# Five slots in place of eight in a ring of gathered expert rows

## The reference, cut to what matters

```python
def peer_ffn(xn, wq, keys1, keys2, u_tab, v_tab):
    q = (xn @ wq).reshape(t, PEER_HEADS, PEER_D_KEY)
    s1 = jnp.einsum('thd,hkd->thk', q[..., :half], keys1)
    s2 = jnp.einsum('thd,hkd->thk', q[..., half:], keys2)
    v1, i1 = lax.top_k(s1, PEER_TOPK)
    v2, i2 = lax.top_k(s2, PEER_TOPK)
    cand = (v1[..., :, None] + v2[..., None, :]).reshape(t, PEER_HEADS, PEER_TOPK * PEER_TOPK)
    cs, ci = lax.top_k(cand, PEER_TOPK)
    ...
    expert = e1 * PEER_N_KEYS + e2
    gate = jax.nn.softmax(cs, axis=-1)
    ...
        act = jax.nn.gelu(jnp.einsum('td,thkd->thk', xb, u_tab[eb]), approximate=False)
        return jnp.einsum('thk,thkd->td', gb * act, v_tab[eb])
```

## Time and profile before

| | |
|---|---|
| median of 3 runs | 4342.82 us (4341.18 to 4344.03) |
| the profiled execution | 4336.71 us, span 4334.8 us |
| mean granted TensorE clock | 0.953 |
| busy share of the span | PE 83%, DVE 62%, ACT 36%, POOL 35% |
| packets of the gathers' queue | 1342.26 MB, 74.7% of 16 engines' span |
| the two expert layers | from 643.4 us to 2587 us, and from 3018 us to 4317.5 us |

### The profile page before, as it was taken

The page is one execution under the profiler, slowest core; times in us unless marked ns, Lnnn a source line. Parts: engine busy times, 40 slices in busy tenths (PEclk is TensorE's granted clock), DMA queues, the critical chain, the costliest instruction groups (busy, mean ns, idle before and its releaser), DMA issues. The chain is left out here.

```text
span 4334.8 us, 33292 instructions
## 1 busy us (share of the span) xinstructions
PE 3589.7 (83%) x10024; PEld 1674.6 (39%) x10024; DVE 2684.7 (62%) x6235; ACT 1564.1 (36%) x4522; POOL 1536.3 (35%) x1338
## 2 busy tenths in 40 slices
PE   8899989778778778779777768997877877877776
PEld 1289563233233223223222227785332322322222
DVE  2221349785875875875875445664987587587444
ACT  1121014344334334334333332552444433433333
POOL 0101304444444444444444321000454444444442
PEclk9899599999999999999999999998999999999999
DMA  8712029999999999999999982003999999999998
GB/s 309 267 59 88 0 109 421 403 421 421 421 419 421 415 410 422 416 415 420 414 415 422 421 359 72 4 1 132 421 400 421 421 421 420 420 409 415 422 421 338
DMA packets 232988, 1455.27 MB, mean 336 GB/s; under 512 B 25140, under 2 KB 25140, under 8 KB 67812
## 3 DMA queue, kind: packets, MB, share of 16 engines
q0 software_dynamic: 184320, 1342.26, 74.7%
q1 hardware_dynamic: 48392, 110.79, 7.2%
q10 hardware_dynamic: 96, 0.10, 0.0%
HBM read 1447.72 MB, written 5.34 MB: 335 GB/s over the span
## 5 line engine op out<-in xcount | busy, mean ns | idle before, releaser
L1345 PE MATMUL peer_py<-peer_ring,peer_diag 128*128 128x512 f32 x5120 | 2505.0, 625 | 620.8 <-ACT peer_diag L1275 610.1
L1445 DVE CUSTOM_DVE_ANT_0 peer_ring<-peer_ring,peer_f 128x1024 f32<-128x1024 f32 x1280 | 1556.1, 1224 | 918.6 <-DMA peer_ring<-in_uv_dram,peer_idx 909.9
L1228 POOL DMA_INDIRECT peer_ring<-in_uv_dram,peer_idx x1280 | 1451.7, 1134 | 1817.9 <-PE peer_py L1345 1692.5
L1345 PEld LDWEIGHTS peer_py<-peer_ring,peer_diag 128*128 128x128 f32 x5120 | 929.3, 194 | 2148.7 <-ACT peer_diag L1275 1320.4
L1269 ACT ACTIVATE peer_gel<-peer_u 128x1 f32<-128x1 f32 x1280 | 258.8, 202 | 1827.0 <-DVE peer_u L1445 1825.7
L1275 ACT ACTIVATE peer_diag<-ident,peer_coef 128x128 f32<-128x128 f32 x1280 | 513.8, 401 | 41.7
L1273 ACT ACTIVATE peer_coef<-peer_gel,peer_gate 128x1 f32<-128x1 f32 x1280 | 377.1, 295 | 46.7 <-ACT peer_gel L1269 0.4
L316 DVE TENSOR_TENSOR m_w_low<-m_w_low_plain,m_w_high 128x2048 fp32r<-128x2048 f32 x26 | 61.0, 2347 | 218.1 <-ACT m_w_high L311 218.1
L1219 POOL IOTA peer_iota<- 128x16 f32 x2 | 0.3, 144 | 502.1 <-POOLq L763 361.3
L324 PE MATMUL m_ps<-m_w_high,m_aT_high 128*128 128x512 f32 x416 | 165.5, 398 | 3.3 <-DVE m_v L748 1.6
L1320 PE MATMUL peer_pb<-arena,peer_fT 128*128 128x512 f32 x320 | 164.6, 612 | 2.4 <-ACT peer_fT L1242 2.4
(11 more groups left out here) (189 smaller groups left out, 2732.3 us busy)
## 6 DMA issues: line engine op xcount, KB each, us to landing
arena<-in_ada_w_dram SPq DMA_DIRECT2D x16, 2048.0 KB, 10.3
peer_ring<-in_uv_dram,peer_idx POOLq DMA_INDIRECT x1280, 14.9
mod_rows_sb<-in_ada_w_dram SPq DMA_DIRECT2D x8, 2048.0 KB, 10.3
m_w_low_plain<-in_ev_w_in_dram SPq DMA_DIRECT2D x12, 1024.0 KB, 5.0
arena<-in_peer_wq_dram SPq DMA_DIRECT2D x2, 4096.0 KB, 18.4
mod_rows_sb<-mod_rows SPq DMA_DIRECT2D x7, 1024.0 KB, 7.1
m_w_low_plain<-in_od_w_in_dram SPq DMA_DIRECT2D x6, 1024.0 KB, 5.3
m_w_low_plain<-in_ev_w_out_dram SPq DMA_DIRECT2D x4, 1024.0 KB, 5.0
```

The lines of the kernel that those rows point to most:

```text
L1228: pool.indirect_dma_start(ring[:, n % RING], None, A["uv"], bass.IndirectOffsetOnAxis(idx[:, i % 2, hd, k:k + 1], 0)).then_inc(sem(f"lande ...
L1345: ins = pe.matmul(PY[:, i % 2, b], diag[:, n % RING], ring[:, n % RING, D + b * HALF:D + (b + 1) * HALF], start=s == 0, stop=s == TS - 1)
L1445: dve.tensor_tensor_reduce(x, x, f[:, i % 2], 1.0, 0.0, ALU.mult, ALU.add, u[:, n % RING:n % RING + 1]).then_inc(sem("dot"), 1)
```

## The change

The constant `RING` is 5 in place of 8. With it the ring in SBUF has five entries of 8 KB a partition, and the diagonals and the columns `u`, `gel` and `coef` five entries. There are five semaphores `landed0` to `landed4`. GpSimd waits for the combine of slot `n - 5` where it waited for that of slot `n - 8`. The count, the order and the sizes of the instructions are as before.

```diff
 NH, NK, TOPK = 8, 128, 16
 EXPERTS = NK * NK
-RING = 8
+RING = 5
 LAG = 2
```

## The result

With five slots the kernel takes 4601.53 us (median, 4594.42 to 4604.82), against 4343.42 us (4341.18 to 4344.82) for the kernel before on the same chip: a ratio of 1.0593, 95% interval 1.0574 to 1.0611. It is slower, as forecast, but by 258 us where the forecast was 69, and outside the range.

The account below looks back on a forecast made before the run. The gathers' DMA was taken as the bound through both expert stages. Excess turns over 7.0 us summed to 15 + 12 + 21 + 4 + 5 + 12 = 69 us, giving 4412 us, 1.6% slower; range 4365 to 4475.

Parts of the forecast that it names:

- the queues stay full as long as the turn is no longer than 12.4 - 5.4 = 7.0 us: Five-slot round of 12.4 us less a 5.4 us landing: only turns (landing to reissue) over 7.0 us stop the DMA engines.
- slower quiet tiles: Sign in the last tiles: if they slow down, landing under load exceeds 5.4 us and the whole sum is too small.
- So the two last tiles (2 of 10) lose nothing: Each layer's last, quiet tile: turn of 4.54 us below 7.0, three gathers in flight carry the full rate; no loss.
- The stall in the first tiles: ScalarE waits 12.23 us for the first tile's last index; three more gathers fall into the hole, 7.5 us each time, 15 us.
- The rest of the first tiles: First tiles outside the stall, VectorE busy 110.5 of 117 us, turns 8 to 12 us: 6 us each, 12 us.
- Batches, queries and clock in the middle tiles: Late slots at 16 softmax batches (21 us), six ends of queries on TensorE (4), some 12 slow TensorE clock spells (5).
- GpSimd's own time: Issues take 1134 ns in the mean, 0.937 us in the median; 40 bursts x 0.3, 12 us (0 to 30).
- The other landing time: The skill's 4.4 us landing for 1 MB would allow turns of 8.0 us; the trace's 5.4 was held to contradict it.
- The light case: Rival: late slots overlap more or landing needs under 5.4 us; only turns above 8 cost; +29, 4372 us; chance 0.13.
- the hidden one: Rival: the 9.9 us chain is below 12.4 and lateness is made up; within 9 us, 4343 us; chance 0.04.
- Faster: Rival: with three gathers in flight, less queue contention shortens each gather; 4310 us at 0.08 us less each; chance 0.03.
- Heavy: Rival: TensorE waiting for late gathers drops to 1.2 GHz in routing stretches; 130 us more, 4545 us; chance 0.12.

Follow-up runs that it names:

- wait5_ring8: The kernel before with its eight slots in memory, but GpSimd waits for the combine of slot n-5; 4601.25 us, ratio 1.0602.
- ring4: The kernel with RING set to 4, against the kernel before with eight slots; 5129.99 us, ratio 1.1805.
- the ladders: Two five-slot kernels, one index wait a tile, idle ScalarE copies lengthening the quiet tiles' turn stepwise, dots there from SBUF or PSUM; single executions, 4638.66 and 4608.39 us.
- one_index_wait: Five slots, GpSimd waiting for a tile's indices once, not at each head, except in a layer's first tile; 4577.61 us, ratio 1.0550 to the kernel before.
- the shorter pieces: Five slots, the two longest of a head's four VectorE routing pieces cut in two; 4535.55 us, ratio 1.0431 to the kernel before.
- psum_dots_ring5: Five slots, every dot reading the token's features from PSUM in place of SBUF; 4572.12 us, ratio 1.0530 to the kernel before.
- the other edits: Five slots with one index wait a tile, the later copy of scores in first tiles and the cut routing pieces; 4489.88 us, ratio 1.0328 to the kernel before.
- ring6: The kernel with RING set to 6, against the kernel before with eight slots; 4370.96 us, ratio 1.0066.
- ring9: The kernel with RING set to 9, the most that fit, against the kernel before with eight slots; 4340.30 us, ratio 0.9990.
- four_edits: Five slots, one index wait a tile, later scores in first tiles, cut routing pieces and dots from PSUM; 4447.82 us, ratio 1.0256 to the kernel before.

## Why the prediction was off, point by point

**The bound and the direction: right.** The gathers set the pace and the loss is time in which the DMA engines ran dry; `wait5_ring8` shows that the distance of GpSimd's wait is the cause, all of it within the intervals.

**The step that failed** is "the queues stay full as long as the turn is no longer than 12.4 - 5.4 = 7.0 us". The 5.4 was read from a gather that met 16 idle engines, the one at 775.4. The landings at 684 to 690 took 7.8 to 8.6 us, and I used them only for the rate. Under load `ring4` gives 7.7 us, and the ladders give a limit for the turn of 5.0 (dots from SBUF) to 5.3 us (from PSUM). With the limit at 5.0, 0.5 us above the quiet turn, nearly every late slot counts, and not only bursts over 7.0. The trace before could have told how many: of the 768 slots of its middle tiles 78 have a turn over 7.0 us and 430 one over 5.0. All terms but the stall were too small for that reason, as the prediction itself said that slower quiet tiles would show.

**"So the two last tiles (2 of 10) lose nothing": wrong,** +20 us. Most of it (14 us by `one_index_wait`) is a delay of 0.5 us at each head's start, which puts the issue under a dot and makes 1.97 us of its 0.94.

**The stall in the first tiles, 15 us: right in place and nearly in size.** The wait behind it grew by 8.5 us for the 7.5 worked out, and taking the hole away gave 21 us for both.

**The rest of the first tiles, 12 us: measured about 70** (91 less the 21). **Batches, queries and clock in the middle tiles, 21 + 4 + 5: measured 148,** of which the shorter pieces give back 46. No run isolates the bursts after table loads. The ordinary routing piece of 2.7 to 3.0 us, which holds a dot back and makes a turn of 6.2 us (median, already in the kernel before), had a cost that I put at zero.

**"GpSimd's own time", 12 us (0 to 30): measured 28** (`psum_dots_ring5`), 31 beside the other edits. I took the long issues for noise in the mean. They follow a rule: in both traces an issue that begins from 0.1 to 1.1 us after a dot's start ends 2.03 us after that start (1.95 us long at 0.1, 1.6 at 0.4, 1.25 at 0.8); nearly all others take 0.94. With the dot's second input in PSUM the same issues take 0.94 too. The Trainium skill (SBUF — State Buffer, Who interferes with whom) says that a VectorE instruction with two inputs in SBUF contends with a GpSimd instruction that reads SBUF. The traces agree: the dot has both inputs in SBUF, the gather's issue takes its indices (`peer_idx`) from there, and it is stretched to as much as 1.97 us. The Trainium skill's trap named "DVE blocks DMA" (same page, SBUF: two separate sides) says that GpSimd can't write the descriptors of a DMA while VectorE runs an operation in a 2-port perf mode. Which of the two, reading the indices or writing the descriptors, is held up here no run tells. I had not weighed that page.

**The other landing time.** The estimate of 4.4 us from the Trainium skill (DMA: Bandwidth & Descriptors, Anatomy of one DMA — SWDGE path) is further off under load than my own 5.4. In the quiet tiles the gathers with four and five slots take 7.7 and 7.9 us.

**The rivals.** The light case and the hidden one fall. *Faster* falls too: the DMA engines took more time for the same packets, not less, 74.7% of 4334.8 = 3238 us before and 73.4% of 4596.6 = 3374 after. *Heavy* falls: the mean granted clock is 0.947 for 0.953, and a middle tile has 0.96 for 0.98; no loop between waits and clock is seen. TensorE's combine is busy 57 us longer (2561.7 for 2505.0), and what that adds to the turns was not isolated.

## What to carry to other kernels

The depth that a ring of gathers needs is (turn + landing under load) / interval, and the landing must be taken where few transfers are in flight but the engines are busy, not from one that met idle engines; here (4.5 + 7.7) / 2.49 = 4.9, so five slots have almost no slack, and six lose 0.7%, nearly all of it in the first tiles. With no slack every lateness counts, so a count of the worst bursts is a lower bound and not the sum. And where GpSimd issues the gathers, look at which VectorE operation each issue begins under.

## What the runs showed of the hardware beyond that

**The 16 DMA engines of one gather are not in step.** Each raises the gather's semaphore when its part has landed. From the first of these 16 events to the last, one gather takes 6.0 us before (median), 1.7 after, 1.8 in `ring4`, 2.0 in `ring6` and 8.6 in `ring9`; for the gather at 775.4 it is 0.34. With eight slots the last engine is some 4 us (3.9) behind the last but one. It may be the one that also carries the instruction loads (packets of 16 KB, 1.1 us each): behind several of them its lag grows by about 1 us, from 3.9 to 4.9 behind the one at 2315.8, but not behind each, and the records don't name an engine. A deep ring lets an engine run ahead, and a short one makes all wait for the slowest. That would be a part of why a landing under load is longer than one that meets idle engines, but it is argued, not shown.

**An engine that ran dry starts slowly.** Of the 163840 packets of 8 KB in a run, normally 0.31 us long, 859 take over 0.4 us before, 2092 in `ring6`, 7531 after and 17544 in `ring4`; of the first 16 packets after a pause most take 0.5 to 1.25. The long packets account for the 136 us by which the engines' time grew, 3374 for 3238 us. A late issue is thus followed by slow packets; that this adds to the loss was not isolated by a run.

**What stays open.** Why a landing under load takes 7.7 us where an idle one takes 5.4. How the 111 us that `four_edits` still loses divide between turns held up by routing and these slow starts. And a part of why six slots lose so little: where an issue begins 4.0 to 4.5 us before the landing ahead of it, `ring6` still has intervals of 2.49 us in the median (though only 11 of them), where five slots have 3.26.
